# Operand parts moved to 112 bytes, modulo 256, from the split weights' address, with sixty idle products at the end of TensorE's program

## The chip, the cores and the metric

One NeuronCore of a Trainium2 chip. The metric is the device time of one execution in microseconds (us); a shorter time is better. Times given for a kernel are medians of several executions. A profile is of one execution, taken by the hardware profiler.

## What is computed

A token matrix x of 256 x 1024 floats goes through three transformer layers. The first has a modulation by six vectors of `silu(c) @ w_ada`, a gated depthwise convolution, a multi-scale pooling branch, and a feed-forward part with a depthwise convolution. The second has a gated delta rule (a recurrence over chunks) and a SwiGLU. The third has blockwise attention with rotary positions and a SwiGLU. Each sublayer ends in a layer norm:

```
h  = layer_norm(x) * (1 + sc1) + sh1;  proj = h @ w_in
x  = layer_norm(a1 * x + g1 * mix @ w_out);  x = layer_norm(a1 * x + g2 * (gelu(gt) * v) @ w_down)
x  = layer_norm(a2 * x + gated_deltanet(x));  x = layer_norm(a2 * x + (silu(g) * u) @ w2)
x  = layer_norm(a2 * x + moba_attention(x));  x = layer_norm(a2 * x + (silu(g) * u) @ w2)
```

Nearly all of the arithmetic is the product of 256 tokens with weight matrices in float32, about 199 MB of them, each read once.

## The kernel before

**Units.** The weights come from HBM in 356 loads of 128 x 1024 floats (512 KB), in the order of `PLAN` (line 95). 48 of them (`ada`) are used by VectorE alone, three are used as they are, the others are *units*: each is a block of 128 contraction rows by 1024 outputs, or eight 128 x 128 blocks that make one output tile.

**Three products for one.** A float32 product is made of three products of the type float32r, which TensorE takes in one pass. Weights and operand are each split into a high part (rounded to float32r) and a low part (the rest). `three` (line 629) issues high x high, high weights x low operand, low weights x high operand, all accumulated in one PSUM bank; line 632 is its matmul. The weights' parts are `hi` and `lo`, five slots each of 1024 floats; ScalarE writes `hi` from `raw` (line 1300), VectorE writes `lo` as `raw - hi` (line 1899). The operand's parts are `hh` and `hl` (eight blocks of 128 x 256, for every layer's input) and `fh` and `fl` (four blocks, for the feed-forward parts' inner activations).

**Which of the two moves.** Each matmul has a stationary side, which a weight load (LDWEIGHTS, 128 columns) brings in ahead, and a moving side, which is streamed. `tile` (line 635), `rows_in` (line 669), `first_tiles` (line 654) and `gdn_tile` (line 1052) keep a block of weights stationary and move 256 tokens of the operand: rows of the trace with `128x256`. `rows_out_of` (line 872), `tokens_unit` (line 902) and `z` (line 1021) pass `flip=True`: 128 tokens of the operand are stationary, and 512 columns of `hi` or `lo` move: rows with `128x512`. In a row's `out<-in` the moving operand and the stationary one stand in the order in which the program names them in the instruction: `ps<-hh,hi` with 128x256 moves `hh` against `hi`; `ps<-hi,fh` with 128x512 moves `hi` against `fh`.

**Order of work.** TensorE runs its program in the order written: 4584 products that move `hh` or `hl`, 528 that move `fh` or `fl` (the first layer's down projection, by `rows_in`), 1104 that move `hi` or `lo`, and some 1280 others: transposes, the delta rule, attention. The products of one kind follow each other in blocks of 12, 24 or 48. The last work is `ffn_tokens("w131", ...)` (line 1290), whose last 36 products are `down` projections into banks 0 to 3. VectorE and ScalarE then norm these banks (lines 1868 to 1870 and 2611 to 2633), and the SyncE queue sends out four pieces (line 578).

**Addresses.** The tensors are laid out one after the other in each partition, in the order of lines 353 to 379. Counted in floats, `first` has 184, `dummy` 16, `eps` 24, `raw` 11 x 1024, so `hi` begins at 11488 floats: byte 45952, which is 128 modulo 256. Everything up to `mod` is a multiple of 256 bytes long, so `lo` too is at 128, and so is every slot and block of both. `mod` (48), `ones` (384) and `gap0` (24) put `hh` at byte 88736, or 160 modulo 256: **32 bytes past the weights' remainder**, `hl` and all their blocks too. `gap1` (8 floats) puts `fh` and `fl` at 192: **64 bytes past it**. `idle` and all that follow up to `cst` are at 192. `idle` is a tile of ones; `spin` (line 624) multiplies it with itself, moving 256 columns of it against its own first 128, so there the two are **0 bytes** apart. `spin` serves to keep TensorE running while it has nothing to do.

Of the kernel before, what the change touches and what calls it, by code (L numbers as in the profile page):

```python
# [13 lines left out]
P = 128  # L14
S = 256
# [41 lines left out]
def downs_at(j):  # L57

    return {4: (0, 1), 5: (2, 3), FF - 1: ()}.get(j, (j - 2,))
# [226 lines left out]
class Marks:  # L286
# [21 lines left out]
    def at(self, name, key=0):  # L308
        return self.sem(name), 1 if self.counting else self.place[name, key]
# [33 lines left out]
def program(nc, wts, head, vecs, csts, rows, xtok, xT, low_dram, inv_dram, out):  # L343
    with ExitStack() as ctx:
        def sb(name, shape, dt=F):
            return ctx.enter_context(nc.sbuf_tensor(name, shape, dt))
# [10 lines left out]
        hi = sb("hi", [P, SPLIT, 1024], FR)  # L357
        lo = sb("lo", [P, SPLIT, 1024], FR)
        mod = sb("mod", [P, 48])
        ones = sb("ones", [P, 3, P])  # L360
        gap0 = sb("gap0", [P, 24])
        hh = sb("hh", [P, NC, S], FR)
        hl = sb("hl", [P, NC, S], FR)
        gap1 = sb("gap1", [P, 8])
        fh = sb("fh", [P, 4, S], FR)
        fl = sb("fl", [P, 4, S], FR)
        idle = sb("idle", [P, S], FR)
        crow = sb("crow", [P, D])
        xa = sb("xa", [P, NC, S])
# [10 lines left out]
        bank = [ctx.enter_context(nc.psum_tensor(f"ps{i}", [P, 512], F)) for i in range(8)]  # L380
# [130 lines left out]
        xh = B[5]  # L511
# [109 lines left out]


        def tensor(g, s):
            def spin(n, b=7):
                s.wait_ge(*at("fill", "pad"))
                for _ in range(n):
                    g.matmul(bank[b][:, 0:S], idle[:, 0:P], idle[:, :], start=True, stop=True, skip_group_check=True)
# [121 lines left out]
            for t in range(4):  # L749
                s.wait_ge(*at("tap", (TAPS_V - 1, t)))  # L750
                x = cv[:, t, :].rearrange("p (u v) -> p v u", v=2)
                for v in range(2):
                    a = v * S + t % 2 * P
# [5 lines left out]
            for b in range(2):  # L759
                for v in range(2):  # L760
                    s.wait_ge(*at("norm_v", ("ya", b, v)))
                    for t in (2 * b, 2 * b + 1):
                        a = (t % 2) * S + v * P
# [108 lines left out]
            def rows_out_of(kind, k, xh, xl, made, cs, last, between=None):  # L872

                j = UNIT[kind, k]
                wh, wl = slot(j)
                s.wait_ge(*at(*lo_of(j)))
                s.wait_ge(*made)
                for c in cs:
                    v = slice(c * P, c * P + P)
                    for n in range(2):  # L880
                        m = three(bank[2 * c + n][:, :], wh[:, n * 512:n * 512 + 512], wl[:, n * 512:n * 512 + 512],
                                  xh[:, v], xl[:, v], False, last, flip=True)
                        if between and n == 0:
                            between()
                        if last and kind == "w21" and n == 0:
                            m.then_inc(*up("last_mm", c))
                    if last:
                        m.then_inc(*(up("unit", j) if c else up("tok", kind)))
                if 1 in cs and not last:
                    m.then_inc(*up("unit", j))  # L890
# [36 lines left out]
            def ffn_tokens(kup, kdown, kr, nid, frees, between=None):  # L927

                def down(j, cs):
                    rows_out_of(kdown, j, fh[:, j % 4, :], fl[:, j % 4, :], at("f4_lo", (kup, 1)) if j < 4 else at("f_lo", (kup, j)),  # L930
                                cs, j == FF - 1, between if j == FF - 1 and cs == (1,) else None)

                absorb(kr, nid, frees)
                for k in range(4, 8):
                    tokens_unit(kr, nid, k, 0)
                    tokens_unit(kr, nid, k, 1)
                for j in range(4, FF):
                    for half in (0, 1):
                        t = 2 * j + half
                        tile(kup, j + half * FF, R3[t % 4], nid, at("ff_out", (kup, t - 4)) if t > 11 else  # L940
                             at("f4_lo", (kup, t - 10)) if t > 9 else at("n_a" if half else "n_v", (nid, 7 if half else 3, 0)))
                        if t == 8:
                            for c in range(2):
                                s.wait_ge(*at("f4", (kup, c)))
                                s.wait_ge(*at("n_v", (nid, 3, 1)))
                                s.wait_ge(*at("n_a", (nid, 7, 1)))
                                for i in range(4):
                                    m = g.transpose(bank[6 + c][:, i * P:i * P + P], half_ev[:, c, i * P:i * P + P], ident)
                                m.then_inc(*up("f4_mm", (kup, c)))
                    if j == 4:  # L950
                        for k in range(8):
                            carry_in(nid, k)
                    for d in downs_at(j):
                        down(d, (0, 1))
                for c in range(2):
                    for j in (FF - 3, FF - 2, FF - 1):
                        down(j, (c,))
# [330 lines left out]
                bout(k, (1,))  # L1288

            ffn_tokens("w131", "w21", "w13r1", "x5", x5_free)  # L1290


        def scalar(g, s):
# [1485 lines left out]
```

## Time and profile before

| | |
|---|---|
| median of 3 executions | 1038.99 us (1038.88 to 1039.18) |
| the profiled execution, its own time | 1041.34 us |
| its span, first to last instruction | 1039.5 us |
| TensorE busy with matmuls | 1023.4 us, 98% |
| VectorE, ScalarE, GpSimd busy | 754.0, 572.9, 27.5 us |
| DMA | 201.22 MB, 194 GB/s over the span |

A matmul's busy time in these records is from its start to its end, which includes some 0.16 us of latency that the next one overlaps. So it is the distance between the starts of two products that tells what one costs, and the time a product takes cannot be read from the column of means.

### The profile page before, as it was taken

How to read it: one execution, taken by the hardware profiler on the slowest of the kernel's cores; microseconds unless marked ns; L12 is line 12 of the kernel's file. 1: busy time of each engine (PE TensorE's matmuls, PEld its weight loads, DVE VectorE, ACT ScalarE, POOL GpSimd, SP SyncE). 2: the span in 40 equal slices, each digit the busy share in tenths (PEclk: the TensorE clock that was granted, in tenths of full speed). 3: DMA queues.
4: the chain of work that ended last, by engine and by line, in shares of the span. 5: the costliest groups of instructions: out<-in, count | busy, mean ns of one | idle time of the engine just before them, and what ended most of it. 6: DMA issues, size and time to landing. Idle time of an engine off the chain costs nothing.

```text
span 1039.5 us, 18332 instructions
## 1 busy us (share of the span) xinstructions
PE 1023.4 (98%) x7499; PEld 958.9 (92%) x7499; DVE 754.0 (73%) x1293; ACT 572.9 (55%) x960; POOL 27.5 (3%) x34
## 2 busy tenths in 40 slices
PE   8999999999999999999999999999999999999997
PEld 7999998999999998999987999999899878999996
DVE  6988998899777788877867555555889576555555
ACT  5573447665555586724646445444746565444443
POOL 0000000000100042000000000000000000000000
PEclk9999999999999999999999999999999999999999
DMA  9999873588765533622245555665364426655511
GB/s 370 418 419 370 316 243 124 196 270 274 233 190 193 165 108 115 224 63 80 84 142 186 167 186 191 188 194 186 121 229 158 132 95 250 209 187 183 186 58 41
DMA packets 59603, 201.22 MB, mean 194 GB/s; under 512 B 10496, under 2 KB 10880, under 8 KB 59264
## 3 DMA queue, kind: packets, MB, share of 16 engines
q1 hardware_dynamic: 58368, 199.98, 56.2%
q8 instruction: 60, 0.98, 0.4%
q10 hardware_dynamic: 1152, 0.07, 0.1%
q14 instruction: 23, 0.19, 0.1%
HBM read 198.71 MB, written 1.31 MB: 192 GB/s over the span
## 4 chain that ended last, share of the span: by engine, by line
PE 86%; DVE 10%; ACT 2%; issue 1%; DMA 1%; SPq 0%; DVEq 0%; ACTq 0%
PE ps L632 73%; PE ps L1012 4%; DVE lo L1899 2%; DVE raw L1883 1%; DVE B L2356 1%; PE ps L818 1%; PE ps L720 1%; DVE B L1968 1%; PE ps L771 1%; PE ps L869 1%; DMA B<-in_t 1%; ACT hi L1300 1%; PE ps L806 0%; PE ps L791 0%; DVE sm L2180 0%
## 5 line engine op out<-in xcount | busy, mean ns | idle before, releaser
L1899 DVE TENSOR_TENSOR lo<-raw,hi 128x1024 fp32r<-128x1024 f32 x297 | 360.8, 1222 | 123.3 <-ACT hi L1300 122.6
L632 PE MATMUL ps<-hh,hi 128*128 128x256 f32 x1528 | 432.1, 283 | 2.2 <-DVE hl L1945 1.1
L632 PE MATMUL ps<-hl,hi 128*128 128x256 f32 x1528 | 426.7, 279 | 0.0
L632 PE MATMUL ps<-hh,lo 128*128 128x256 f32 x1528 | 426.7, 279 | 0.0
L1300 ACT ACTIVATE hi<-raw 128x1024 fp32r<-128x1024 f32 x305 | 318.4, 1052 | 50.2 <-PE ps L632 49.1
L632 PEld LDWEIGHTS ps<-hh,hi 128*128 128x128 f32 x1528 | 287.3, 188 | 6.3 <-issue 2.0
L632 PEld LDWEIGHTS ps<-hl,hi 128*128 128x128 f32 x1528 | 287.3, 188 | 1.9 <-issue 0.3
L632 PEld LDWEIGHTS ps<-hh,lo 128*128 128x128 f32 x1528 | 287.3, 188 | 0.0
L632 PE MATMUL ps<-hi,fh 128*128 128x512 f32 x192 | 76.3, 397 | 0.0
L632 PE MATMUL ps<-lo,fh 128*128 128x512 f32 x192 | 75.9, 395 | 0.0
L632 PE MATMUL ps<-hi,fl 128*128 128x512 f32 x192 | 75.8, 395 | 0.0
L632 PE MATMUL ps<-hi,hh 128*128 128x512 f32 x176 | 71.7, 408 | 1.2 <-DVE hl L2202 0.6
L632 PE MATMUL ps<-lo,hh 128*128 128x512 f32 x176 | 69.6, 395 | 0.0
L632 PE MATMUL ps<-hi,hl 128*128 128x512 f32 x176 | 69.5, 395 | 0.0
L1883 DVE CUSTOM_DVE_ANT_0 raw<-raw,crow 128x1024 f32<-128x1024 f32 x48 | 57.9, 1217 | 0.0
L632 PE MATMUL ps<-fh,hi 128*128 128x256 f32 x176 | 48.7, 276 | 0.0
L632 PE MATMUL ps<-fh,lo 128*128 128x256 f32 x176 | 48.6, 276 | 0.0
L632 PE MATMUL ps<-fl,hi 128*128 128x256 f32 x176 | 48.6, 276 | 0.0
L1589 ACT ACTIVATE ev<-ps 128x256 f32<-128x256 f32 x36 | 13.8, 384 | 57.2 <-PE ps L632 57.2
L632 PEld LDWEIGHTS ps<-lo,fh 128*128 128x128 f32 x192 | 36.1, 188 | 8.5
L1509 ACT ACTIVATE ev<-ps,vec 128x256 f32<-128x256 f32 x41 | 22.9, 559 | 37.4 <-PE ps L632 37.4
L1586 ACT ACTIVATE ev<-ps 128x256 f32<-128x256 f32 x36 | 13.8, 383 | 52.8 <-PE ps L632 52.8
(333 smaller groups left out, 1277.4 us busy)
## 6 DMA issues: line engine op xcount, KB each, us to landing
raw<-in_w SPq DMA_DIRECT2D x356, 512.0 KB, 4.3
Z<-in_w SPq DMA_DIRECT2D x9, 512.0 KB, 9.9
B<-in_t SPq DMA_DIRECT2D x2, 512.0 KB, 4.9
B<-in_w SPq DMA_DIRECT2D x2, 512.0 KB, 8.5
h<-in_w SPq DMA_DIRECT2D x2, 512.0 KB, 7.7
xa<-in_x SPq DMA_DIRECT2D x1, 1024.0 KB, 8.6
B<-in_r SPq DMA_DIRECT2D x1, 1024.0 KB, 6.4
out<-h SPq DMA_DIRECT2D x4, 256.0 KB, 2.0
```

The costliest lines, as they stand in the source:

```text
L632: m = g.matmul(o, l, r, start=first and n == 0, stop=last and n == 2, skip_group_check=True)
L720: x = g.matmul(o, (y_odd if half else y_even)[:, t, a:a + P], cw[m % CW_SLOTS][:, n * P:n * P + P].rearrange("p (v n) -> p v n", v=2), sta ...
L771: g.matmul(acc(b0, n), cw[m % CW_SLOTS][:, n * P:n * P + P], x, start=n % 2 == 0, stop=False, skip_group_check=True)
L818: m = g.matmul(bank[UP_BANKS[t]][:, 0:260], raw[:, i % RAW, k * P:k * P + P], rx[:, k, 0:260], start=k == 0, stop=k == 7, skip_group_check ...
L869: g.matmul(bank[2 * c + k // 4][:, (k % 4) * P:(k % 4) * P + P], xa[:, k, c * P:c * P + P], ident, is_transpose=True, start=k % 4 == 0, st ...
L1012: m = g.matmul(bank[b][:, i * P:i * P + P], left(i), right(i), start=i == 0, stop=True, skip_group_check=True)
L1300: g.activation(hi[:, j % SPLIT, :], raw[:, PLACE[j] % RAW, :], ACT.Copy).then_inc(*up("hi", j))
L1509: g.activation(e, p, ACT.Identity, scale=V("w_dw_f", n * 3 + 2), bias=V("b_dw_f", n)).then_inc(*up("tap2", t))
L1586: g.activation(ev[:, t % 4, :], bank[4 + t % 4][:, 0:S], ACT.Copy, scale=1.0 / ALPHA2).then_inc(*up("ff_out", (kup, t)))
L1589: g.activation(ev[:, t % 4, :], bank[4 + t % 4][:, 0:S], ACT.Silu).then_inc(*up("ff_out", (kup, t)))
L1883: g.tensor_tensor_reduce(r, r, crow[:, :], 1.0, 0.0, ALU.mult, ALU.add, mod[:, col:col + 1]).then_inc(*up("ada", n))
L1899: g.tensor_tensor(lo[:, j % SPLIT, :], raw[:, PLACE[j] % RAW, :], hi[:, j % SPLIT, :].bitcast(F), ALU.subtract).then_inc(*up("lo", j))
```

## The change

It does two things. The gaps between tensors are resized: `gap0` from 24 to 44 floats, `gap1` from 8 to 52, and `gap1` goes behind `fl`. `hh` then begins at byte 88816, `fh` at 105200, both 240 modulo 256. All four operand parts are so **112 bytes past the weights' remainder** (or the weights 144 past theirs). `idle` and what follows move on by 256 bytes and keep their remainder modulo 256. And behind the last unit TensorE gets 60 more matmuls, `idle_rows` five times: each moves 256 columns of `hh` or `hl`, from a start shifted by 12, 16, 20, 24 or 28 floats, against blocks of `hi` and `lo` of slot 0, into bank 4, which nobody reads. (They are so 160, 176, 192, 208 and 224 bytes past the weights' remainder.) They wait for nothing. `idle_wide` is defined and not called.

```diff
-        gap0 = sb("gap0", [P, 24])
+        gap0 = sb("gap0", [P, 44])
         hh = sb("hh", [P, NC, S], FR)
         hl = sb("hl", [P, NC, S], FR)
-        gap1 = sb("gap1", [P, 8])
         fh = sb("fh", [P, 4, S], FR)
         fl = sb("fl", [P, 4, S], FR)
+        gap1 = sb("gap1", [P, 52])
         idle = sb("idle", [P, S], FR)
...
+            def idle_rows(shift, n, by=0):
+                xh, xl = (x[:, :, :].rearrange("p a b -> p (a b)") for x in (hh, hl))
+                for k in range(n):
+                    a = k * S + shift
+                    w = k % 4 * P + by
+                    three(bank[4][:, 0:S], hi[:, 0, w:w + P], lo[:, 0, w:w + P], xh[:, a:a + S], xl[:, a:a + S], True, True)
...
             ffn_tokens("w131", "w21", "w13r1", "x5", x5_free)
+            idle_rows(12, 4)
+            idle_rows(16, 4)
+            idle_rows(20, 4)
+            idle_rows(24, 4)
+            idle_rows(28, 4)
```

## Rows read from the trace of the kernel before

**Rows 1.** The page, part 1: busy time, share and instructions of each engine.

```profile
PE 1023.4 (98%) x7499; PEld 958.9 (92%) x7499; DVE 754.0 (73%) x1293; ACT 572.9 (55%) x960; POOL 27.5 (3%) x34
```

**Rows 2.** The page, part 4: the chain that ended last.

```profile
PE 86%; DVE 10%; ACT 2%; issue 1%; DMA 1%; SPq 0%; DVEq 0%; ACTq 0%
PE ps L632 73%; PE ps L1012 4%; DVE lo L1899 2%; DVE raw L1883 1%; DVE B L2356 1%; PE ps L818 1%; PE ps L720 1%; DVE B L1968 1%; PE ps L771 1%; PE ps L869 1%; DMA B<-in_t 1%; ACT hi L1300 1%; PE ps L806 0%; PE ps L791 0%; DVE sm L2180 0%
```

**Rows 3.** TensorE's timeline: hh and hl moving, 61 products from the first row to the last.

```profile
749.36 0.28 PE L632 MATMUL ps<-hh,lo 128*128 128x256 f32 x1
...
756.36 0.28 PE L632 MATMUL ps<-hh,lo 128*128 128x256 f32 x1
```

**Rows 4.** TensorE's timeline: fh and fl moving, the second and the last of 24.

```profile
293.16 0.28 PE L632 MATMUL ps<-fl,hi 128*128 128x256 f32 x1
...
295.65 0.28 PE L632 MATMUL ps<-fh,lo 128*128 128x256 f32 x1
```

**Rows 5.** TensorE's timeline: idle moving against itself; instructions and timeline.

```profile
L627 PE MATMUL ps<-idle x18: 279/283/363, 14.1 to 16.2; 128*128 128x256 f32 x18
...
14.06 2.39 PE L627 MATMUL ps<-idle 128*128 128x256 f32 x18
```

**Rows 6.** TensorE's timeline: hi and lo moving against hh and hl, 28 products.

```profile
850.03 0.40 PE L632 MATMUL ps<-lo,hh 128*128 128x512 f32 x1
...
856.33 0.40 PE L632 MATMUL ps<-lo,hh 128*128 128x512 f32 x1
```

**Rows 7.** TensorE's timeline: hi and lo moving against fh and fl, the last 36 products.

```profile
1024.27 0.39 PE L632 MATMUL ps<-hi,fh 128*128 128x512 f32 x1
...
1032.42 0.39 PE L632 MATMUL ps<-lo,fh 128*128 128x512 f32 x1
```

**Rows 8.** Engines by stretch: length, busy us (instructions) of each engine, clock, DMA share, GB/s.

```profile
core 0: us, PE busy (x) PEld busy (x) DVE busy (x) ACT busy (x) POOL busy (x), PEclk, DMA share, GB/s
23.45:65.69 42.24, 42.24 (x361) 42.24 (x362) 40.48 (x65) 27.52 (x44) 0.00 (x0) 1.00 1.03 418
66.59:92.16 25.57, 25.57 (x213) 25.26 (x213) 22.22 (x43) 11.74 (x21) 0.00 (x0) 1.00 1.03 418
92.16:127.48 35.32, 34.22 (x287) 33.19 (x287) 31.62 (x64) 13.91 (x24) 0.00 (x0) 1.00 0.87 336
130.97:162.44 31.47, 31.47 (x259) 31.06 (x258) 27.76 (x56) 15.46 (x26) 0.00 (x0) 1.00 0.75 263
198.24:357.67 159.43, 159.43 (x1376) 159.43 (x1377) 130.72 (x197) 95.95 (x145) 4.04 (x5) 1.00 0.70 224
424.12:530.00 105.88, 105.78 (x892) 103.94 (x892) 81.35 (x153) 52.65 (x105) 0.00 (x0) 1.00 0.33 101
578.92:731.33 152.41, 152.41 (x1064) 141.45 (x1063) 80.95 (x89) 75.31 (x108) 0.00 (x0) 1.00 0.58 187
741.96:797.00 55.04, 55.04 (x433) 53.27 (x434) 48.32 (x85) 32.12 (x57) 0.00 (x0) 1.00 0.58 191
876.19:1032.16 155.97, 155.97 (x1078) 144.31 (x1078) 81.68 (x95) 74.48 (x108) 0.56 (x1) 1.00 0.45 142
```

**Rows 9.** Products of line 632 by form in the fifth stretch, 198.24 to 357.67 us.

```profile
L632 PE MATMUL ps<-hh,hi x296: 277/280/357, 198.2 to 351.0; 128*128 128x256 f32 x148
...
L632 PE MATMUL ps<-fh,hi x163: 276/276/282, 201.1 to 357.5; 128*128 128x256 f32 x163
```

**Rows 10.** The chain of waits in order of time, whole execution: start, us, what.

```profile
66.59 2.80 PE ps L632 x24
...
109.28 1.58 DVE B L1968 x4
...
870.76 0.87 PE ps L948 x8
```

**Rows 11.** The last stretch of the timeline, all engines but TensorE.

```profile
1031.34 6.13 SPq L578 DMA_DIRECT2D out<-h  x4
...
1036.42 0.69 DVE L2633 TENSOR_TENSOR h<-h,B 128x512 f32<-128x512 f32 x1
```

More of the change, by code:

```diff
@@ L623, in tensor, with idle_wide @@
         def tensor(g, s):
+            def idle_rows(shift, n, by=0):
[4 more added lines that the diff above has]
+                    three(bank[4][:, 0:S], hi[:, 0, w:w + P], lo[:, 0, w:w + P], xh[:, a:a + S], xl[:, a:a + S], True, True)
+            def idle_wide(shift, n, by=0):
+                xh, xl = (x[:, :, :].rearrange("p a b -> p (a b)") for x in (hh, hl))
+                for k in range(n):
+                    a = k * S + shift
+                    three(bank[5][:, :], hi[:, 0, by:by + 512], lo[:, 0, by:by + 512], xh[:, a:a + P], xl[:, a:a + P], True, True,
+                          flip=True)
             def spin(n, b=7):
```

## The prediction

> **What bounds the kernel now.** I read the page's busy shares first: TensorE is busy 98% of the span, VectorE 73%, ScalarE 55% [rows 1]. Busy TensorE alone proves little, since one product's time overlaps the next's, so the second view is the chain that ended last: 86% of it is TensorE, 73% the matmuls of line 632, 10% VectorE [rows 2]. The kernel is as long as these products stand apart. The third view gives that distance. The granted clock is at its full level, 2.4 GHz, in every stretch used here [rows 8].
>
> - 256 columns of `hh` or `hl`, 32 bytes past the weights' remainder: 60 distances in 756.36 - 749.36 = 7.00 us, **116.7 ns** each [rows 3].
> - 256 columns of `fh` or `fl`, 64 bytes past: 22 distances in 295.65 - 293.16 = 2.49 us, **113.2 ns** [rows 4].
> - 256 columns of `idle` against itself, 0 bytes apart: 18 products in 2.39 us; without the last one's 0.28, 17 distances in 2.11 us, 124 ns, and less the 0.08 us by which the first is longer (363 against 283 ns), **119.4 ns** [rows 5].
> - 512 columns of `hi` or `lo` against `hh` or `hl`, the moving side 32 bytes behind: 27 distances in 6.30 us, **233.3 ns** [rows 6]; against `fh` and `fl`, 64 bytes behind: 35 in 8.15 us, **232.9 ns** [rows 7].
>
> Same shape, clock and type, other distances: I take it that a moving stream and the weight load beside it get in each other's way, by how their addresses stand to each other. From 0 to 32 to 64 bytes a 256-column product falls by 2.7 and 3.5 ns.
>
> **What the products will cost at 112 bytes.** No row shows 112, so it is bounded. Carried on at 3.3 ns per 32 bytes, the line gives 113.2 - 1.5 x 3.3 = 108.2 ns. Below the shortest distance in the trace it should not go: eight transposes of 128 columns stand 0.87 / 8 = 109 ns apart, where a weight load is also issued for each [rows 10]. So the lower end is 109. The upper end is outside what is seen: if 112 is really 16 short of a repeat at 128, it is like 0 or worse, 119.4 to 121. I take **109.4**, next to the line's end, since three rows lie on the line and none against it. That is 7.3 ns less for `hh` and `hl`, 3.8 less for `fh` and `fl`.
>
> For the 512-column products the moving side goes from 32 and 64 behind to 112 behind (144 ahead, modulo 256). The two rows differ by 0.4 ns only, so there the address seems not to matter, and I take **no change**. Bounds: down to 2 x 109 = 218 ns, 15 less; up by the same 3.3 ns per 32 bytes from 64 to 112, 5 more.
>
> **The sum.** A shorter distance counts only where TensorE's products lead the chain. Stretches of rows 8, with counts of the 256-column products from the order of the program (24 for a tile):
>
> 1. 23 to 66 us, 361 products: 361 x 7.3 = 2.6, but VectorE is busy 40.5 of the 42.2 us, so at most 42.2 - 40.5 = **1.8**. The DMA share is 1.03 there; no product waits for a load, though, and the eleven slots of `raw` stand between.
> 2. 66 to 92 us, five tiles, of which one is shown, 2.80 us [rows 10]: 120 x 7.3 = **0.9**.
> 3. 92 to 127 us: the chain is VectorE's (line 1968 is one of its pieces [rows 10], 31.6 us busy of 35.3): **0**.
> 4. 131 to 162 us, ten tiles: 240 x 7.3 = **1.8**.
> 5. 198 to 358 us, 3 x 296 = 888 on `hh` and 3 x 163 = 489 on `fh` [rows 9]: 888 x 7.3 + 489 x 3.8 = 6.5 + 1.9 = **8.3**. VectorE is busy 130.7 of 159.4 us and 151.1 remain.
> 6. 424 to 530 us, sixteen tiles: 384 x 7.3 = **2.8**.
> 7. 579 to 731 us, 34 tiles: 816 x 7.3 = **6.0**.
> 8. 742 to 797 us, sixteen tiles: **2.8**; VectorE 48.3 of then 52.2 us.
> 9. 876 to 1032 us, 34 tiles: **6.0**. Two tiles just before the seventh and ninth: **0.4**.
>
> Together 30.8 us.
>
> **The idle products.** The last product that counts starts at 1032.42 and holds the array 0.23 us [rows 7]. Sixty more at 109 to 120 ns take 6.5 to 7.2 us, and the last needs another 0.17 us for its latency: 1039.4 to 1040.0. Meanwhile VectorE's last piece starts at 1036.42 and the four output transfers hold their queue until 1031.34 + 6.13 = 1037.47 [rows 11]; the span ends at 1039.5. So nearly all of it lies beside the tail, which is the cover; without it the price would be 7. Bank 4 and slot 0 are wanted by nobody then, no instruction is queued behind them on TensorE, and they wait for none. Cost: -0.0 to +0.6, taken as **+0.3**.
>
> The profiled execution's own time is 1041.34, its span 1039.5. 1041.3 - 30.8 + 0.3 = 1010.8. That execution stood 2.35 above the median of the runs, so the median should be **1008.5 us**.
>
> **A rule against it.** The trace shows two distances, 116.7 and 113.2 ns, for one shape, one clock and one weight side [rows 3, 4]. The Trainium skill says in "TensorE: Matmul & The Clock Gate", Part 2, step by step, that TensorE reads the moving side and the weights through two independent ports, and that loading the next weights takes no bandwidth from the running matmul; "SBUF — State Buffer", "Who interferes with whom", says that TensorE never waits on anyone. By that rule addresses would be free of cost and only the idle products would be left, 1039.3. Rows 3 to 5 speak against it.
>
> **Rivals.**
>
> - *The wide products gain too* (0.17). 144 ahead could be as clear of the load as 112 is: 1104 x 15 ns = 16.6 us more, about 992. For it: they stand 15 ns above twice the shortest distance. Against it: rows 6 and 7 are alike.
> - *The fall stops at 64 bytes* (0.12). Then `hh` goes to 113.2, 3.5 ns less on 3696 products outside the first stretch, 12.9, and 1.3 in the first, nothing for `fh`: 1038.99 - 14.2 + 0.3 = 1025.
> - *The wide products lose* (0.09): 1104 x 5 = 5.5 us: 1014.
> - *The pattern repeats every 128 bytes* (0.12), the slow side. 112 then stands 16 before a repeat, and the place is the weight load beside each 256-column product. At 119.4 to 120 ns it costs 3 ns on 4584 products (13.8 us) and 6.5 on 528 (3.4): 1039 + 17 + 0.3 = 1056. It decides from where the new distance is over 116.7 ns: 112 bytes need only lie past the line's turn. Against it: the fall from 0 to 64 would have to turn within 48 bytes more.
> - *Nothing happens* (0.04): the 3.5 ns are not the address but the kind of unit, since `fh` moves in `rows_in` only, into alternating banks. Against it: the first 361 products on `hh` are also `rows_in`, and 42.24 / 361 = 117.0 ns [rows 8]. 1039.3. The rule above comes to the same and is in this chance.
>
> **How the numbers follow.** The forecast has 0.46. 0.2% (2.1 us) is about what a measurement of this kernel can tell from no change. Faster: 0.46 + 0.17 + 0.12 + 0.09 = 0.84; within 0.2%: 0.04; slower: 0.12. The range takes in the first four cases with the ends of their costs: from 992 less 4 for what the line's end and slack could add, 988, to 1025 plus 3 for waits that appear as TensorE gets faster (VectorE is busy 130.7 us in the fifth stretch), 1028. It leaves out 0.16.
>
> **What would show it.** Right: `hh,hi` with 128x256 starting 109 to 110 ns apart, `fh,hi` alike, so that the two can no longer be told apart; the chain still TensorE's, its stretch from 198 us some 8 us shorter, those from 579 and 876 us 6 each; `hi,fh` with 128x512 at 233 ns; 60 products on bank 4 after the last unit, ending within 0.6 us of the last output. Wrong: a distance over 113 ns for `hh`, another for 512 columns than 233, or a stretch whose products stand closer and which is no shorter, with waits for line 1899 (`lo`) or line 1300 (`hi`) in it. The idle products will also show 160 to 224 bytes, twelve each.

## The result and the profile after

The changed kernel takes **1047.7 us** (median of 4 executions, 1047.56 to 1048.2); the kernel before takes 1039.09 on the same chip (4 executions, 1038.88 to 1039.61). The ratio is **1.0083**, 95% interval 1.0066 to 1.0101: slower by 8.6 us. Forecast were 1008.5 and a range up to 1028, so the number, the sign and the range were all wrong. The profiled execution's own time is 1048.2, its span 1046.4. That is only 6.9 over the 1039.5 of before, because TensorE was slow at the start of the profile of before: its granted clock from 10 to 14 us was 0.57 there and 1.00 here.

The page of the kernel after: busy shares, then the chain that ended last, by engine (the lines beyond 590 have moved: 632 is 646, 1899 is 1918, 1300 is 1319).

```profile
PE 1039.1 (99%) x7559; PEld 976.3 (93%) x7559; DVE 752.5 (72%) x1293; ACT 574.2 (55%) x960; POOL 27.5 (3%) x34
PE 90%; DVE 7%; ACT 2%; issue 1%; DMA 0%; SPq 0%; ACTq 0%; DVEq 0%
```

Against [rows 1, 2] TensorE leads more of the chain, 90% for 86, and VectorE less, 7% for 10. So there is no new wait: TensorE has become slower. Its timeline says by how much. From first to last row these are 24 products on `fh` and `fl`, 61 on `hh` and `hl`, and the last 36 of 512 columns.

```profile
294.72 0.28 PE L646 MATMUL ps<-fh,hi 128*128 128x256 f32 x1
...
297.45 0.28 PE L646 MATMUL ps<-fh,lo 128*128 128x256 f32 x1
...
753.43 0.28 PE L646 MATMUL ps<-hl,hi 128*128 128x256 f32 x1
...
760.55 0.28 PE L646 MATMUL ps<-hl,hi 128*128 128x256 f32 x1
...
1030.58 0.39 PE L646 MATMUL ps<-hi,fh 128*128 128x512 f32 x1
...
1038.71 0.40 PE L646 MATMUL ps<-lo,fh 128*128 128x512 f32 x1
```

For `hh`, 60 distances in 7.12 us are **118.7 ns**, where [rows 3] gave 116.7. For `fh`, 23 in 2.73 us are **118.7**, where [rows 4] gave 113.2. 35 in 8.13 us are 232.3, where [rows 7] gave 232.9. The mean over all blocks is 118.7 for the first two. `hh` and `fh` can indeed no longer be told apart, as the forecast had it, but at 118.7 and not at 109.4.

The windows table over the stretches that answer to four of [rows 8]; columns as there.

```profile
21.58:64.54 42.96, 42.96 (x361) 42.96 (x362) 40.66 (x65) 27.83 (x44) 0.00 (x0) 1.00 1.03 418
92.16:127.48 35.32, 34.48 (x287) 33.45 (x287) 31.78 (x65) 13.89 (x24) 0.00 (x0) 1.00 0.86 335
197.81:363.23 165.42, 165.41 (x1394) 165.42 (x1395) 133.39 (x203) 98.74 (x147) 4.04 (x5) 1.00 0.68 219
581.52:735.51 153.99, 153.99 (x1063) 143.27 (x1063) 81.00 (x89) 75.32 (x108) 0.00 (x0) 1.00 0.58 184
```

The clock is 1.00 as before. The first stretch is 0.7 us longer for the same products, the seventh (581 us) 1.6: 816 x 2.0 ns = 1.6. The fifth (198 us) runs on for 18 products more; without these (2.1 us) it is 3.9 longer, against 888 x 2.0 + 489 x 5.5 = 4.5 worked out. The third, VectorE's, holds the same 287 products. Over the kernel: 4584 x 2.0 = 9.2, 528 x 5.5 = 2.9, 1104 x (-1) = -1.1, idle products +0.5, 11.5 in all. What the two traces show is less. The 251st matmul of the program starts at 38.70 us before and at 37.08 after, the last one that counts at 1032.42 and at 1038.71: 7.9 us longer between the same two, and with the tail 8.5, which is the 8.6 of the medians. Part of what the sum has too much lies where TensorE does not lead: from the 3001st matmul to the 3251st the kernel before takes 33.9 us and the changed one 32.6.

The tail in the timeline: the output transfers, the first idle product, VectorE's last piece, the last idle product:

```profile
1037.64 6.12 SPq L578 DMA_DIRECT2D out<-h  x4
...
1038.95 0.28 PE L646 MATMUL ps<-hh,hi 128*128 128x256 f32 x1
...
1042.71 0.69 DVE L2652 TENSOR_TENSOR h<-h,B 128x512 f32<-128x512 f32 x1
...
1045.88 0.28 PE L646 MATMUL ps<-hh,lo 128*128 128x256 f32 x1
```

The sixty idle products run beside VectorE's and the queue's work to 1046.16, 0.24 before the span's end. From the start of the last product that counts to the end it is 1046.4 - 1038.71 = 7.7 us, before 1039.5 - 1032.42 = 7.1.

The sixty products also say at which distances they stand. These are the 6th and the last of the second twelve, then the 4th and the last of the third twelve.

```profile
1040.95 0.28 PE L646 MATMUL ps<-hh,lo 128*128 128x256 f32 x1
...
1041.63 0.28 PE L646 MATMUL ps<-hh,lo 128*128 128x256 f32 x1
...
1042.10 0.28 PE L646 MATMUL ps<-hh,hi 128*128 128x256 f32 x1
...
1043.05 0.28 PE L646 MATMUL ps<-hh,lo 128*128 128x256 f32 x1
```

0.68 / 6 = 113.3 ns and 0.95 / 8 = 118.8 ns. By the sums of sizes they stand at 176 and 192 bytes. The scan below has 119.5 ns at 176, 113.4 at 192 and 119.5 at 208, so they behave as if they stood 16 bytes further on.

### The profile page after: what moved, and what is told of

The parts are those of the page before. It is cut to its first block, busy times and chain, and to the rows that moved or that the text cites. A ratio compares the mean times of both kernels' runs of the same rounds, so it can differ in the third digit from the quotient of the medians.

```text
span 1046.4 us, 18452 instructions
## 1 busy us (share of the span) xinstructions
PE 1039.1 (99%) x7559; PEld 976.3 (93%) x7559; DVE 752.5 (72%) x1293; ACT 574.2 (55%) x960; POOL 27.5 (3%) x34
## 3 DMA queue, kind: packets, MB, share of 16 engines
q10 hardware_dynamic: 1152, 0.07, 0.1%
## 4 chain that ended last, share of the span: by engine, by line
PE 90%; DVE 7%; ACT 2%; issue 1%; DMA 0%; SPq 0%; ACTq 0%; DVEq 0%
PE ps L646 77%; PE ps L1026 4%; DVE lo L1918 2%; DVE raw L1902 1%; PE ps L832 1%; PE ps L734 1%; DVE B L1987 1%; PE ps L785 1%; PE ps L883 1%; PE ps L805 1%; ACT hi L1319 0%; PE ps L820 0%; DMA B<-in_t 0%; DVE sm L2199 0%; PE ps L1250 0%
## 5 line engine op out<-in xcount | busy, mean ns | idle before, releaser
L646 PE MATMUL ps<-hh,hi 128*128 128x256 f32 x1548 | 441.1, 285 | 2.0 <-DVE hl L1964 1.2
L646 PE MATMUL ps<-hl,hi 128*128 128x256 f32 x1548 | 435.8, 282 | 0.0
L646 PE MATMUL ps<-hh,lo 128*128 128x256 f32 x1548 | 435.6, 281 | 0.0
L646 PEld LDWEIGHTS ps<-hh,hi 128*128 128x128 f32 x1548 | 291.6, 188 | 6.0 <-issue 1.7
L646 PEld LDWEIGHTS ps<-hl,hi 128*128 128x128 f32 x1548 | 291.6, 188 | 2.1 <-issue 0.3
L646 PEld LDWEIGHTS ps<-hh,lo 128*128 128x128 f32 x1548 | 291.5, 188 | 0.0
L1608 ACT ACTIVATE ev<-ps 128x256 f32<-128x256 f32 x36 | 13.8, 384 | 58.6 <-PE ps L646 58.6
L1605 ACT ACTIVATE ev<-ps 128x256 f32<-128x256 f32 x36 | 13.8, 383 | 54.7 <-PE ps L646 54.7
```

The costliest lines, as they stand in the source:

```text
L646: m = g.matmul(o, l, r, start=first and n == 0, stop=last and n == 2, skip_group_check=True)
L1605: g.activation(ev[:, t % 4, :], bank[4 + t % 4][:, 0:S], ACT.Copy, scale=1.0 / ALPHA2).then_inc(*up("ff_out", (kup, t)))
L1608: g.activation(ev[:, t % 4, :], bank[4 + t % 4][:, 0:S], ACT.Silu).then_inc(*up("ff_out", (kup, t)))
```

## The experiments

All 17 runs are told, in the order in which they ran. Medians stand against 1039.1 to 1039.2 for the kernel before in the same set, unless another is given. "Spacing" is the mean distance between the starts of products in the timeline, after the first few of a block.

### The two parts alone

`e1_addr_only` is the changed kernel without the five calls.

```diff
-            idle_rows(12, 4)
...
-            idle_rows(28, 4)
```

> The new addresses without the sixty idle products. Theory A (the address makes the loss): products on hh stay at 118.8 ns as in the changed kernel, the idle products cost only what they add behind the output, 0.4 to 0.8 us, so 1047 us, 8 us above the kernel before. Rival B (the idle products make the loss, for example by holding up the last transfers): back to 1039 to 1040 us.

Measured: 1047.46 (1047.14 to 1050.8), ratio 1.0092 (1.0073 to 1.011). `e2_idle_only` has the five calls and the gaps of before.

```diff
-        gap0 = sb("gap0", [P, 44])
+        gap0 = sb("gap0", [P, 24])
+        gap1 = sb("gap1", [P, 8])
         fh = sb("fh", [P, 4, S], FR)
         fl = sb("fl", [P, 4, S], FR)
-        gap1 = sb("gap1", [P, 52])
```

> The addresses of before with the sixty idle products. Theory A: 1039.4 to 1039.9 us, products on hh at 116.7 ns as before, and only the end of the span is later, by 0.4 to 0.8 us. Rival B: 1045 us or more.

Measured: 1039.89 (1038.07 to 1040.37), 1.0005 (0.9996 to 1.0015). So nearly the whole loss is the addresses', and the idle products cost 0.2 (1047.7 against 1047.46) to 0.7 us (1039.89 against 1039.21).

### Spacing against distance

`e3_scan` adds products behind the last unit of the kernel before, into banks 4 and 5, which nobody reads: 24 of 256 columns and then 12 of 512 for each of 16 distances, by shifting a slice of `hh`, `hl` in steps of 16 bytes.

```diff
+            def scan_rows(shift, by, n):
+                xh, xl = (x[:, :, :].rearrange("p a b -> p (a b)") for x in (hh, hl))
+                for k in range(n):
+                    a, w = k % 4 * S + shift, k % 4 * P + by
+                    three(bank[4][:, 0:S], hi[:, 0, w:w + P], lo[:, 0, w:w + P], xh[:, a:a + S], xl[:, a:a + S], True, True)
...
+            for shift in range(0, 64, 4):
+                scan_rows(shift, 0, 8)
+            for shift in range(0, 64, 4):
+                scan_wide(shift, 0, 4)
```

> The kernel before with a scan behind the last unit: 24 products of 256 columns of hh and hl at each of sixteen distances from 32 to 272 bytes past the weights, in steps of 16, then 12 products of 512 columns of hi at each of sixteen distances of hh. Theory A1 (a function of the distance modulo 256 alone): 116.7 ns at 32, 113.3 at 64, 118.8 at 112, 113.4 at 176 and near 119 at 160 and 192, and 272 like 16. Theory A2 (a repeat every 128 bytes): 32 like 160, 48 like 176, 64 like 192. Rival C (the distance is not what counts, but what precedes a product): no steady value by distance, scatter of the same size inside each block. The 512-column products: A says 231 to 234 ns throughout, as at the three distances seen.

The scan's timeline: the 4th and the last product of the blocks at 96, 112, 128 and 192 bytes, 20 distances each.

```profile
1042.23 0.28 PE L644 MATMUL ps<-hh,hi 128*128 128x256 f32 x1
...
1044.63 0.28 PE L644 MATMUL ps<-hh,lo 128*128 128x256 f32 x1
...
1045.10 0.28 PE L644 MATMUL ps<-hh,hi 128*128 128x256 f32 x1
...
1047.36 0.28 PE L644 MATMUL ps<-hh,lo 128*128 128x256 f32 x1
...
1047.83 0.28 PE L644 MATMUL ps<-hh,hi 128*128 128x256 f32 x1
...
1050.20 0.28 PE L644 MATMUL ps<-hh,lo 128*128 128x256 f32 x1
...
1059.19 0.28 PE L644 MATMUL ps<-hh,hi 128*128 128x256 f32 x1
...
1061.46 0.28 PE L644 MATMUL ps<-hh,lo 128*128 128x256 f32 x1
```

2.40, 2.26, 2.37 and 2.27 us over 20 are 120.0, 113.0, 118.5 and 113.5 ns. All blocks, in ns (a row of 512 columns counts the weights as the side that moves, `hh` so many bytes ahead of it):

```
bytes   32    48    64    80    96   112   128   144   160   176   192   208   224   240   256   272
 256  116.7 118.3 117.8 119.8 119.9 113.4 118.5 118.7 117.3 119.5 113.4 119.5 118.4 116.8 119.7 118.5
 512  233.0 233.3 233.0 232.3 234.3 233.4 234.0 233.6 233.0 229.1 228.4 233.3 233.3 226.7 226.7 226.7
```

There is no line from 32 to 64 bytes. The spacings lie between 113.3 and 120 ns in no order of distance; 113.3, 116.7, 117.8, 118.7 and 120 ns come back in later runs, and others (117.3 at 160 bytes, 119.5 at 176) stand between them. The best one shows at two distances, **112 and 192**. And at 112, where the changed kernel's parts were meant to be, a product costs 5.4 ns less than it does in the changed kernel. That contradiction was to be explained. At 64 bytes the scan has 117.8, where `fh` in [rows 4] has 113.2: the distance is not all of it either.

`e4_all64` puts all four parts at 64 bytes.

```diff
-        gap0 = sb("gap0", [P, 24])
+        gap0 = sb("gap0", [P, 32])
-        gap1 = sb("gap1", [P, 8])
```

> The gaps resized so that hh and hl, too, lie 64 bytes past the weights, fh and fl as before, no idle products; all tensors behind them keep their very addresses. Theory A (distance decides): products on hh at 113.3 instead of 116.7 ns, 3.4 ns on some 3700 products that lead the chain, 12 to 14 us less, 1025 to 1027 us. Rival D (the 113.3 ns of fh belongs to its kind of unit or its place, not to the 64 bytes): hh stays at 116 to 117 ns and the time within 1 us of before.

Measured: 1044.4 (1044.35 to 1045.23), 1.0057 (1.0042 to 1.0072). Its timeline, 61 products from first to last row, in its first stretch and in a later one:

```profile
29.76 0.28 PE L631 MATMUL ps<-hl,hi 128*128 128x256 f32 x1
...
36.56 0.28 PE L631 MATMUL ps<-hl,hi 128*128 128x256 f32 x1
...
750.76 0.28 PE L631 MATMUL ps<-hl,hi 128*128 128x256 f32 x1
...
757.83 0.28 PE L631 MATMUL ps<-hl,hi 128*128 128x256 f32 x1
```

6.80 us over 60 are 113.3, 7.07 are 117.8. One program, one distance, **two steady spacings**. The first holds for the 408 products of its first block (14.5 to 60 us) and for 96 from 184 us on; nearly all else has the second, `fh` too, whose address has not moved against the weights. So neither expectation came true. The kernel before has both spacings on `fh` as well. These are the first and the last product of the `fh` block that starts at 201 us:

```profile
201.12 0.28 PE L632 MATMUL ps<-fh,hi 128*128 128x256 f32 x1
...
203.83 0.28 PE L632 MATMUL ps<-fh,lo 128*128 128x256 f32 x1
```

2.71 / 23 = 117.8 ns, in the stretch where [rows 4] has 113.2.

`e5_fine_up` and `e6_fine_down` take the scan of 256 columns in steps of 4 bytes, upwards and downwards (before: 1037.48 us in that set).

```diff
-            for shift in range(0, 64, 4):
+            for shift in range(0, 64):
                 scan_rows(shift, 0, 8)
```

> The kernel before, and behind the last unit 24 products of 256 columns of hh and hl at each of 64 distances, 32 to 284 bytes past the weights in steps of 4, rising, with no pause between. Theory A (the distance alone sets the spacing): one curve, which the falling scan repeats; 64, 112 and 192 bytes as in the coarse scan, 117.8, 113.4 and 113.4 ns. Theory S (each distance has a few steady spacings, out of 113.3, 116.7, 117.8, 118.7 and 120 ns, and the products before a block decide which one it falls into): at some distances the value differs from the coarse scan's, where a block was entered from 16 bytes less and not from 4. Some 180 us longer than before.

```diff
-            for shift in range(0, 64, 4):
+            for shift in range(63, -1, -1):
                 scan_rows(shift, 0, 8)
```

> The same 64 distances, falling. Theory A: the same value at each distance as rising, to within 0.5 ns. Theory S: a quarter or more of the distances differ by over 1 ns from the rising scan, and both values are steady within their block.

Measured, one execution each, 1214.68 and 1214.72 us: with 1536 products added. The mean of the 16 distances that are multiples of 16 bytes is 117.4 ns (up) and 118.3 (down), that of the 48 others 120.0 and 119.8, the worst 123.4 (at 132 bytes up, at 260 down). The best level came on the way up at 144 (113.3) and 192 (113.6); on the way down these two had 118.7 and 117.8. At 112 both ways came down to 113.3 by the end of the block (means 114.6 and 115.9). So the distance alone does not set the level of a block, and 112 is where it fell to the best either way. Whether the order of the scan makes the difference, one execution of each does not show: `e16_all192_again` below has two levels in one program.

`e7_entries` asks that directly: 48 products at 64, 112, 192 and 32 bytes, each after five different things.

```diff
+            for shift in (8, 20, 40, 0):
+                for kick in range(5):
...
+                    elif kick == 3:
+                        scan_wide(0, 0, 4)
+                    else:
+                        for i in range(8):
+                            g.transpose(bank[6][:, i % 4 * P:i % 4 * P + P], nt[:, 0, i * P:i * P + P], ident)
+                    scan_rows(shift, 0, 16)
```

> Behind the last unit of the kernel before, 48 products at 64, 112, 192 and 32 bytes, each distance entered in five ways: after 12 products at 32 bytes, after 12 at 0, after 12 at 48, after 12 of 512 columns, after 8 transposes. Theory A: five equal values at each distance. Theory S: at 64 bytes 113.3 ns after products at 32 bytes, as the feed-forward blocks of the kernel before show, and 117.8 after products at 48 bytes or after transposes; at 112 bytes 113.3 after some and 118.8 or 120 after others; at 32 bytes 116.7 after most.

Measured, 1175.56 us, in ns (before: 1037.48):

```
bytes   after 12 at 32, 12 at 0, 12 at 48, 12 wide   after 8 transposes
  64                117.8 (all four)                      113.3
 112                113.3 (all four)                      113.3
 192                113.3 (all four)                      113.3
  32                116.7 (all four)                      117.8
```

At 112 it takes about 11 products until the spacing is there, at 192 none to 6. 64 bytes gave 113.3 only after the transposes. So what stands directly ahead can matter at 64 bytes. It does not explain [rows 4]: there the 113.2 ns at 64 bytes come right behind products at 32, and here, after 12 at 32, it is 117.8. The expectation had 113.3 for that entry.

### Layouts taken from the scan

`e8_all192`, `e9_all240` and `e10_all16` set one distance for all parts, by the sizes of two gaps: none and 32 floats, 12 and 20, 20 and 12. (Their names and expectations speak of the distance by the sum of sizes.)

```diff
-        gap0 = sb("gap0", [P, 24])
-        gap1 = sb("gap1", [P, 8])
...
+        gap1 = sb("gap1", [P, 32])
         idle = sb("idle", [P, S], FR)
```

> All four operand parts at 192 bytes past the weights (no gap before hh), all else at its very address, no idle products. The scan behind the last unit gave 113.3 ns at 192 bytes for 256 columns in six of eight blocks, and 228 to 229 for 512 columns. Theory P (what the scan shows at the end carries over to the body): 256 columns at 113.3, 512 at 229, some 13 + 4 us less, 1022 us. Theory Q (in the body a distance falls into another of its steady spacings than at the end, as 112 bytes did): 256 columns at 117.8 or more, 1040 to 1048 us.

Measured: **1026.07** (1025.15 to 1034.34), 0.989 (0.9852 to 0.9928), faster than before by 1%. Its timeline, 61 products on `hh` at 748 us and 24 on `fh` at 293 us:

```profile
748.02 0.28 PE L631 MATMUL ps<-hh,hi 128*128 128x256 f32 x1
...
754.82 0.28 PE L631 MATMUL ps<-hh,hi 128*128 128x256 f32 x1
...
293.26 0.28 PE L631 MATMUL ps<-fh,hi 128*128 128x256 f32 x1
...
295.97 0.28 PE L631 MATMUL ps<-fh,lo 128*128 128x256 f32 x1
```

113.3 ns (6.80 / 60) in the one, 117.8 (2.71 / 23) in the other, which holds for nearly all products from 130 to 358 us. Wide products have 228.9 to 229.5, for 232.8 to 233.2 before. This profile is of the slowest of the four executions, 1034.34 us; the other three took 1025.15 to 1026.28.

```diff
+        gap0 = sb("gap0", [P, 12])
...
+        gap1 = sb("gap1", [P, 20])
```

> All four at 240 bytes. At the end 117.0 ns for 256 columns and 226.7 for 512. Theory P: hh 0.3 ns dearer and fh 3.7, 512 columns 6.4 ns cheaper: + 1 + 2 - 7, 1035 us. Theory Q: 256 columns at 118 to 120 ns, 512 at 233: 1045 us.

Measured: 1053.74 (1053.31 to 1054.17), 1.0139 (1.0122 to 1.0156). Its timeline, 61 products and the last 36 wide ones:

```profile
758.95 0.28 PE L632 MATMUL ps<-hl,hi 128*128 128x256 f32 x1
...
766.14 0.28 PE L632 MATMUL ps<-hl,hi 128*128 128x256 f32 x1
...
1036.55 0.40 PE L632 MATMUL ps<-hi,fh 128*128 128x512 f32 x1
...
1044.51 0.39 PE L632 MATMUL ps<-lo,fh 128*128 128x512 f32 x1
```

119.8 ns (7.19 / 60), and 227.4 (7.96 / 35). The scan had 116.8 at 240 and 119.7 at 256, so this kernel behaves as if at 256, or 0.

```diff
+        gap0 = sb("gap0", [P, 20])
...
+        gap1 = sb("gap1", [P, 12])
```

> All four at 16 bytes (256 less than the 272 of the scan). At the end 116.6 ns (rising) or 118.5 (falling) for 256 columns, 226.7 for 512. Theory P: 1034 to 1042 us, with 512 columns at 226.7. Theory Q: 512 columns at 233 and 1040 us or more.

Measured: 1041.3 (1039.44 to 1042.87), 1.0022 (1.0012 to 1.0031), spacing 116 to 118 and 233: what 32 bytes give.

### Where the parts really lie

`e11_like_main` repeats, behind the last unit of the changed kernel without its idle products, the sequences of the main body, in six forms (accumulation over 12 or 24 products, one slot or five, other banks), each twice, each after eight transposes.

```diff
+            for ks, slots, b, runs, long in ((range(4), (0,), 4, 8, False), (range(8), (0,), 4, 4, False), (range(8), (0,), 4, 4, True),
+                                             (range(8), (1,), 4, 4, True), (range(8), (0, 1, 2, 3, 4), 4, 5, True), (range(4), (2,), 5, 8, True)):
+                for _ in range(2):
+                    reset()
+                    like(ks, slots, b, runs, long)
```

> The changed addresses (112 bytes) without the idle products, and behind the last unit blocks of 96 to 120 products on hh, each after eight transposes and each twice: first as the scan had them (four blocks of hh, slot 0, every group of three closed), then eight blocks of hh, then eight with a sum over all of them as a tile has, then the same from slot 1, from slots 0 to 4 in turn, and four blocks from slot 2 into another bank. The body has 118.7 to 120 ns at this distance and the scan 113.3. Theory F (the form of the sequence chooses the spacing): one of the steps turns 113.3 into 118.7 and names it. Theory G (the work of the other engines beside it chooses): all of them come to 113.3 within 15 products, since VectorE and ScalarE are idle there.

Measured: 1193.66. Two pieces of its chain, one of the first form and one of the fifth:

```profile
1039.61 11.39 PE ps L643 x96
...
1137.74 14.24 PE ps L643 x120
```

11.39 / 96 and 14.24 / 120 are both 118.7 ns, and so it is in all twelve: neither accumulation, slot nor bank matters here, and transposes ahead do not bring 113.3. What is left is the address itself. The distances in this kernel repeat 115, 118, 121, 120, 119 ns over and over, as do those of the scan's block at **128** bytes. So I read the start addresses in the compiled programs' tables of allocations (bytes in a partition; the distance from `hi`, modulo 256, in brackets):

```
                 hi       hh            fh
before        47104    89888 (32)   106304 (64)
after         47104    89984 (128)  106368 (128)
e4_all64      47104    89920 (64)   106304 (64)
e8_all192     47104    89792 (192)  106176 (192)
e9_all240     47104    89856 (0)    106240 (0)
e10_all16     47104    89888 (32)   106272 (32)
```

Every tensor in them starts at a multiple of 32 bytes. (1152 bytes stand ahead of the first one, so all addresses worked out from sizes were that much too low; distances between tensors do not change by it.) `gap0` with 44 floats is 176 bytes long, 5.5 times 32; it starts at 89792 and ends at 89968, and `hh` starts at 89984. **The change puts the parts at 128 bytes, not at 112**, and the idle products at 176, 192, 208, 224 and 240. The gaps of before (96 and 32 bytes) are multiples of 32, so there the distances were right. The 113.3 and 118.8 ns of the idle products above fit 192 and 208 bytes, where the scan has 113.4 and 119.5.

### The change as it is worded

To have 112, one tensor `ops` takes all the parts at 96 bytes, and the parts are its slices from 16 bytes on.

```diff
-        gap0 = sb("gap0", [P, 24])
-        hh = sb("hh", [P, NC, S], FR)
-        hl = sb("hl", [P, NC, S], FR)
-        gap1 = sb("gap1", [P, 8])
-        fh = sb("fh", [P, 4, S], FR)
-        fl = sb("fl", [P, 4, S], FR)
+        gap0 = sb("gap0", [P, 40])
+        ops = sb("ops", [P, 4 + 24 * S], FR)
+        hh, hl, fh, fl = (ops[:, 4 + a * S:4 + b * S].rearrange("p (a b) -> p a b", b=S) for a, b in ((0, 8), (8, 16), (16, 20), (20, 24)))
+        gap1 = sb("gap1", [P, 48])
```

> The four operand parts as views of one tensor that starts at 96 bytes, each view 16 bytes in: a true 112, no idle products. Theory T (the changed kernel has its parts at 128 bytes because tensors start at multiples of 32; 112 itself is a fast distance): 256-column products at 113.3 ns on hh and fh, 512-column ones unchanged at 233, some 14 us less than before, 1024 to 1026 us. Theory Q (the body has another steady spacing than the end): 118.7 ns and 1047 us.

Measured: **1031.75** (1029.16 to 1032.89), 0.9926 (0.9913 to 0.9939): faster than before, by half of what was expected. The profile is of its fastest execution. Its page, the chain by engine:

```profile
PE 84%; DVE 11%; ACT 3%; issue 1%; POOL 0%; DVEq 0%; ACTq 0%; POOLq 0%
```

Its timeline, two rows 60 products apart (all parts are called `ops` here):

```profile
740.03 0.39 PE L630 MATMUL ps<-ops,hi 128*128 128x256 f32 x2
...
746.83 0.39 PE L630 MATMUL ps<-ops,hi 128*128 128x256 f32 x2
```

And its chain in order of time, the pieces of the fifth, seventh and ninth stretch:

```profile
194.36 156.01 PE ps L630 x1374
...
569.13 151.70 PE ps L630 x1062
...
864.73 155.20 PE ps L630 x1077
```

6.80 / 60 = 113.3 ns. The fifth stretch is 156.01 us for [rows 8]'s 159.43, the seventh and ninth 0.7 and 0.8 shorter, so little because the wide products have a mean of 235.7 in them, 3.1 more than before. That is what entering a block costs there, and not the steady spacing. The 1st, 3rd and 12th of twelve wide products behind products of 256 columns:

```profile
591.23 0.66 PE L630 MATMUL ps<-hi,ops 128*128 128x512 f32 x2
591.73 0.39 PE L630 MATMUL ps<-lo,ops 128*128 128x512 f32 x1
...
593.83 0.39 PE L630 MATMUL ps<-lo,ops 128*128 128x512 f32 x1
```

The first two distances are 0.50 us together, the other nine 2.10 / 9 = 233.3 ns, as before the change. The 256-column blocks there pay for the entry too: 14 or 15 of their 48 products pass before 113.3 is reached.

`e13_true112_idle` is the same with the change's sixty products.

```diff
+            idle_rows(12, 4)
...
+            idle_rows(28, 4)
```

> The change as its words have it: a true 112 and the sixty idle products behind the last unit (now at 160, 176, 192, 208 and 224 bytes). Theory T: 0.3 to 0.8 us above the kernel without them, 1025 to 1027 us. Theory Q: 1047 to 1048 us.

Measured: 1032.97 (1031.92 to 1033.53), 0.9938 (0.9924 to 0.9952). So the change as its words have it gains 6 us, where the kernel that was run loses 8.6.

`e14_112_192` has `hh`, `hl` at 112 and `fh`, `fl` at 192, `e15_192_112` the other way round.

```diff
+        ops = sb("ops", [P, 4 + 16 * S], FR)
+        hh, hl = (ops[:, 4 + a * S:4 + b * S].rearrange("p (a b) -> p a b", b=S) for a, b in ((0, 8), (8, 16)))
+        gapm = sb("gapm", [P, 16])
         fh = sb("fh", [P, 4, S], FR)
```

> hh and hl at a true 112, fh and fl at 192. If each pair's own distance sets its cost: hh at 113.3 ns, fh at 113.3 or 117.8, hi and lo against fh at 228 to 229 ns (576 products, 2 to 3 us less than at 112), against hh at 233: 1022 to 1025 us. If entry matters more: fh at 117.8 and hh thrown out of 113.3 behind it in the first feed-forward part, 1028 us or more.

```diff
-        gap0 = sb("gap0", [P, 24])
...
+        gapm = sb("gapm", [P, 40])
+        ops = sb("ops", [P, 4 + 8 * S], FR)
+        fh, fl = (ops[:, 4 + a * S:4 + b * S].rearrange("p (a b) -> p a b", b=S) for a, b in ((0, 4), (4, 8)))
```

> The other way about: hh and hl at 192, fh and fl at a true 112. If each pair's own distance sets its cost: hi and lo against hh at 228 to 229 ns, against fh at 233, hh at 113.3 in the parts where it had that with all four at 192 and, if the blocks at 112 between bring it there, in the first feed-forward part too: 1021 to 1024 us. If not, 1026 us, as with all four at 192.

Measured: 1029.12 (1026.69 to 1030.66), 0.9899 (0.9883 to 0.9915), and 1030.01 (1029.78 to 1032.69), 0.9917 (0.9903 to 0.9931). Mean spacings of four of these kernels, in ns (without distances over 280 ns, "all 192" from the 1034.34 us execution); from 580 us on, blocks of 256 and of 512 columns take turns:

```
                             before    all 192   all 112   112, 192
 24 to 66 us, 256 columns     116.7     113.6     113.6      113.6
198 to 345 us, 256 columns    115.9     117.8     113.3      114.4
580 to 730 us, 256 columns    116.7     113.9     115.0      114.4
580 to 730 us, 512 columns    232.6     228.8     235.7      229.0
```

The mixed layout takes the better one for each: 112 for `hh`, which moves, and 192 for `fh`, which stands still from 580 us on while the weights move.

The two best ran once more, unchanged: `e16_all192_again` is `e8_all192`, `e17_112_192_again` is `e14_112_192`.

> All four parts at 192 bytes once more. If its first result holds: 1025 to 1027 us, 1.1 to 1.3% less than before, with single runs up to 1034. If that was a matter of the chip: 1030 us or more.

> hh and hl at a true 112, fh and fl at 192 once more: 1027 to 1031 us, 2 to 4 us above all four at 192 if the first results hold.

Measured: 1028.44 (1024.9 to 1035.04), 0.9906 (0.988 to 0.9933), and **1028.54** (1028.14 to 1028.91), 0.9896 (0.9882 to 0.991). They can't be told apart by their medians. The mixed one spread by 0.8 us here and by 4 in its first set, all at 192 by 10 and 9. The profile of `e16_all192_again` is of an execution of 1028.93 us. The same 24 products on `fh` that `e8_all192` has from 293.26 on:

```profile
290.30 0.28 PE L631 MATMUL ps<-fh,hi 128*128 128x256 f32 x1
...
292.91 0.28 PE L631 MATMUL ps<-fh,lo 128*128 128x256 f32 x1
```

2.61 / 23 = 113.5 ns, for 117.8 there. From 24 to 66 us it is the other way round, 117.7 ns in the mean for 113.6. **One program settles at different levels in two executions.** From the 1501st matmul to the 3001st `e16_all192_again` takes 172.9 us and `e8_all192` 179.0. It is 0.7 us behind where that begins and 5.4 ahead where it ends, and the two run alike from there on: the 5.4 us between the two profiled executions are these levels. So neither the addresses nor the order of the program fixes the level at 192 bytes.

## Why the prediction was wrong

**What bounds the kernel** held. In every layout the time follows the spacing of these products: from 1026.07 to 1053.74 us with nothing changed but addresses. That also settles what the prediction drew from two pages of the Trainium skill, "TensorE: Matmul & The Clock Gate" (Part 2, step by step: two independent ports) and "SBUF — State Buffer" (Who interferes with whom: TensorE waits on no one). By what it drew, these kernels would take the same time, and they differ by 2.7%. Whether it is the two reads that get in each other's way, as the prediction took it, no run shows.

**The addresses: the step that failed first.** "All four operand parts are so 112 bytes past", from a sum of sizes. They lie at 128. The prediction named "nothing happens" as the way in which a change may not do what it says, and took it for a change without effect; that it might do something else was no case. The runs that show it are `e1_addr_only` against `e12_true112`: 1047.46 at 128 bytes, 1031.75 at 112. (`idle` and what follows moved by 32 bytes between these two as well, which is taken up below.)

**The price at the address: the step that failed next.** "Three rows lie on the line and none against it." Even at true 112 bytes the forecast of 1008.5 is 23 us too low, and 1031.75 lies outside the range. Three things were wrong in it.

- *The line.* The values at 0, 32 and 64 bytes (119.4, 116.7, 113.2) are not points of a slope: 48 bytes, between two of them, has 118.3 in the scan, and 64 has 117.8 or 113.3 in one and the same kernel. Three points from two tensors and a spin loop fitted a line by chance. (Their mean step is 3.1 ns per 32 bytes, not 3.3; that moves the line's end by 0.3 ns.)
- *The floor.* 109 came from transposes of 128 columns. No block of 256-column products in any run settled under 113.3 ns, 272 cycles at 2.4 GHz, and no 512-column one under 226.7, 544 cycles. [Rows 4] itself already stood at that floor.
- *The settling.* From 580 us on the blocks are 48 products long, between wide ones, and at 112 some 14 pass before 113.3 is reached (11 in `e7_entries`). So `hh` had 115.0 and not 113.3 there.

With the measured floor the prediction's own sum for 112 would have been: `hh` 3.4 ns on 3696 products, 12.6, and 1.2 us in the first stretch; `fh` nothing; the wide ones, 234.4 for 233.0 ns in the mean over the kernel, 1.4 x 1104 = 1.5 lost: 1039.1 - 13.8 + 1.5 = 1026.8, 5 under the measurement. Settling is left out of it. The mean of all 256-column products in the profile of `e12_true112` is 114.2 and not 113.3, 0.9 x 3696 = 3.3 us, which leaves 1.6 unexplained. The prediction's rival "the fall stops at 64 bytes", 1025, was the right case for the address it spoke of, all but settling and the loss on the wide products.

**The wide products.** "No change" nearly held for the changed kernel (-1 ns). As a rule it did not: 226.7 to 235.7 ns over the layouts, and the bounds of 15 less and 5 more held all of them.

**The slow-side rival** "the pattern repeats every 128 bytes" had the sign and the place, with 1056 for 1047.7. It was mis-sized as it took 119.4 to 120 for 128 bytes, the level of 0; 128 has its own, 118.7. Its reason was wrong too: 0 and 128 are unlike in the scan, 119.7 and 118.5 ns, and so are 64 and 192.

**The idle products.** +0.3 forecast, bounds 0 to 0.6; measured 0.2, 0.7 and 1.2 in three pairs (the last is `e13_true112_idle` against `e12_true112`, whose executions spread by 1.6 and 3.7 us), and 7.7 for 7.1 us of tail in the profile. The cover, VectorE's norms and the output transfers, was read rightly.

**VectorE next.** VectorE leads 10% of the chain in [rows 2], 11% with all at 112, 12% and 10% in the two profiles with all at 192; that is the slack that the first and fifth terms allowed for, and it did not decide.

What stays open is what sets the levels. The runs show that the address of the operand parts against the weights, modulo 256, picks a set of them; which one of the set comes differs with what ran ahead (`e7_entries`) and, at 192 bytes, between two executions of one program. Which part of the memory or of the engine makes the levels, no run here tells. `hi` and `lo` never moved in these runs. That the distance counts, and not the operand's own address, rests on two things: `spin`, whose tile stands at 64 or 96 bytes and at distance 0, has 120 ns like the scan at 256 and `e9_all240` at 0; and the wide products change with the address of `hh`, which is stationary there, while `hi` and `lo`, which move, stay where they are. A run with the weights moved was not made. `idle`, `Z` and what follows stand at 96 bytes in the changed kernel for 64 before, and that costs next to nothing: `e10_all16` has them at 96 too and is 2.2 us above before, of which `fh` at 116.7 for 113.2 ns is 528 x 3.5 = 1.8.

## What to carry to other kernels

Read a tensor's address from the compiled program before arguing about it: a size that is not a multiple of 32 bytes moved the next tensor by 16 bytes here and turned a gain of 6 to 7 us into a loss of 8 to 9. Where products of one shape stand at two distances in a trace, the alignment of the moving side to the stationary one may be worth 1% of a kernel bound by them; find the good value by a scan on the chip, behind the last work, and then confirm it in the body, over several executions and more than one profile, since a block may settle at another level there, and at another one the next time. And take the floor of a cost from rows of the same shape and type, not from the shortest row of another.

## What was not expected of the hardware

- A stream of float32r products with a weight load each settled at steady spacings between 113.3 and 120 ns for 256 columns, all at a granted clock of 1.00, where the parts were a multiple of 16 bytes apart. It stayed there for hundreds of products, and one program held two of them at one distance (113.3 and 117.8 in `e4_all64` and `e8_all192`).
- Distances that are not multiples of 16 bytes were worse by 1.6 to 2.6 ns in the mean (`e5_fine_up`, `e6_fine_down`), 123.4 ns at worst. The Trainium skill's "SBUF — State Buffer" speaks of lines of 16 bytes in SBUF and of a penalty for an access that crosses into a new one (Door 1: The DMA port swizzle); the two scans agree in direction, and do not show that this is the cause.
- Two executions of one program at 192 bytes settled differently in the same stretch, 117.8 and 113.3 ns. Its times spread by 9 and 10 us, those of the layouts with `hh` at 112 by 0.8 to 4. The two levels account for 5.4 us of it, by the two profiles; that they make all of the spread was not shown.
